# Second layer's recurrence of a hybrid decoder step: key product one slot earlier, output scores in 128-row products, half of the swapping moved to ScalarE

## The reference

```python
def step(s, inp):                      # per token, per head; s is (value, key)
    r_t, lw_t, k_t, v_t, kk_t, a_t = inp
    s_kk = jnp.einsum('bhik,bhk->bhi', s, kk_t)
    s = (s * jnp.exp(lw_t)[:, :, None, :]
         - s_kk[..., :, None] * (kk_t * a_t)[..., None, :]
         + v_t[..., :, None] * k_t[..., None, :])
    return s, jnp.einsum('bhij,bhj->bhi', s, r_t)
```

## Time and profile before

| | |
|---|---|
| median of 3 runs | 1917.25 us (1915.13 to 1920.38) |
| profiled execution | 1919.97 us, span 1918.2 us |
| TensorE busy | 1760.8 us (92%) |
| VectorE busy | 1004.5 us (52%) |
| ScalarE busy | 731.3 us (38%) |
| granted TensorE clock, mean | 0.932 |
| recurrence of layer 2 | about 1089 to 1307 us of the span |

### The profile page before, as it was taken

One profiled execution on the slowest core, in us unless ns is written; L12 is line 12 of the kernel. 1 busy time (PEld: TensorE's weight loads), 2 busy tenths in 40 slices (PEclk: granted clock), 3 DMA queues, 4 the chain that ended last, 5 costly groups with the idle time before them and its releaser, 6 DMA issues.

```text
span 1918.2 us, 42954 instructions
## 1 busy us (share of the span) xinstructions
PE 1760.8 (92%) x18617; PEld 1668.0 (87%) x18617; DVE 1004.5 (52%) x1471; ACT 731.3 (38%) x969; POOL 186.5 (10%) x211
## 2 busy tenths in 40 slices
PE   7999878799999999997999877768899999999997
PEld 6999876799999999996888767765599999999997
DVE  4476774654433444456788556633744442444443
ACT  4353353355522223333466123322445531222343
POOL 1042550000000000110060000012100000000000
PEclk8999988899999999998999867777899999999998
DMA  4322141333332333321222200010143332223321
GB/s 129 89 67 56 47 118 34 88 111 87 92 97 65 87 87 102 103 76 31 69 77 68 67 3 4 4 35 14 28 104 116 87 106 77 70 87 100 87 67 58
DMA packets 234669, 138.95 MB, mean 72 GB/s; under 512 B 4720, under 2 KB 229360, under 8 KB 234528
## 3 DMA queue, kind: packets, MB, share of 16 engines
q1 hardware_dynamic: 226784, 116.73, 21.3%
q0 software_dynamic: 4864, 15.90, 3.3%
q10 hardware_dynamic: 2880, 4.21, 0.6%
HBM read 128.66 MB, written 8.16 MB: 71 GB/s over the span
## 4 chain that ended last, share of the span: by engine, by line
PE 79%; DVE 10%; ACT 5%; issue 3%; POOL 1%; DMA 1%; ACTq 0%; DVEq 0%; SPq 0%; POOLq 0%
PE ps L351 61%; PE ps L2496 2%; PE ps L1881 2%; PE ps L1628 1%; DVE w_rest L320 1%; ACT w_head L315 1%; PE ps L1862 1%; PE ps L1169 1%; POOL mix L984 1%; PE ps L1093 1%; DVE odd_quad L2648 1%; PE ps L2468 1%; PE ps L2775 1%; PE ps L1900 1%; POOL mix L985 0%
## 5 line engine op out<-in xcount | busy, mean ns | idle before, releaser
L351 PE MATMUL ps<-x_split,w_head 128*128 128x272 f32 (+1 forms) x5312 | 897.5, 291 | 25.7 <-DVE x_split L1418 8.5
L351 PEld LDWEIGHTS ps<-x_split,w_head 128*128 128x128 f32 x5312 | 761.4, 191 | 39.8 <-issue 27.4
L351 PE MATMUL ps<-x_split,w_rest 128*128 128x272 f32 (+1 forms) x2656 | 554.3, 290 | 0.0
L315 ACT ACTIVATE w_head<-w_raw 128x1024 fp32r<-128x1024 f32 (+1 forms) x205 | 227.2, 1108 | 582.0 <-PE ps L351 565.4
L351 PEld LDWEIGHTS ps<-x_split,w_rest 128*128 128x128 f32 x2656 | 419.9, 191 | 0.0
L320 DVE TENSOR_TENSOR w_rest<-w_raw,w_head 128x1024 fp32r<-128x1024 f32 (+1 forms) x205 | 268.2, 1308 | 174.3 <-ACT w_head L315 174.2
L351 PE MATMUL ps<-hidden_split,w_head 128*128 128x272 f32 x1408 | 233.1, 287 | 0.0
L351 PEld LDWEIGHTS ps<-hidden_split,w_head 128*128 128x128 f32 x1408 | 198.0, 188 | 0.0
L351 PE MATMUL ps<-hidden_split,w_rest 128*128 128x272 f32 x704 | 145.3, 287 | 0.0
L1459 DVE TENSOR_TENSOR hT<-hT,ps 128x544 f32<-128x544 f32 (+1 forms) x40 | 28.8, 721 | 161.2 <-PE ps L351 161.2
L351 PEld LDWEIGHTS ps<-hidden_split,w_rest 128*128 128x128 f32 x704 | 110.0, 188 | 0.0
(11 more groups left out here) (453 smaller groups left out, 2139.5 us busy)
## 6 DMA issues: line engine op xcount, KB each, us to landing
w_raw<-in_w_ffn_gate SPq DMA_DIRECT2D x44, 512.0 KB, 3.8
w_raw<-in_w_ffn_up SPq DMA_DIRECT2D x44, 512.0 KB, 3.8
w_raw<-in_w_ffn_down SPq DMA_DIRECT2D x32, 704.0 KB, 4.6
w_raw<-in_w_in_even SPq DMA_DIRECT2D x29, 512.0 KB, 3.8
w_raw<-in_w_ple_gate SPq DMA_DIRECT2D x16, 512.0 KB, 4.0
w_raw<-in_w_out_even SPq DMA_DIRECT2D x8, 512.0 KB, 3.9
w_raw<-in_rw_wr SPq DMA_DIRECT2D x8, 512.0 KB, 4.0
w_raw<-in_rw_wk SPq DMA_DIRECT2D x8, 512.0 KB, 3.9
```

Of the source, the lines that this page charges most:

```text
L315: act.activation(wh[:, s, 0:kt * P], raw[:, s, 0:kt * P], ACT.Copy).then_inc(head_ok[s], 1)
L351: mm = pe.matmul(ps[:, 2 * s + h, 0:half.stop - half.start], w[:, s, k * P:(k + 1) * P], x[:, k, half], start=first and k == 0, stop=k == ...
```

## The change

Four things in the recurrence:
- The order of parts is changed. Stream n+2's `aT` is put into slot 1, ahead of U, and its P4 into slot 2. Stream 0 gets one part before the turns of the head begin.
- `O` is 16 products whose stationary tile is 64 rows by 128 columns (both key kinds at once) in place of 32 of 64 by 64.
- The heads' two column halves change places in the inverse tiles (`swap_cols`, `bank(1 - c)`). ScalarE writes the row-swapped half of the inverse beside it (`swapped`), in two copies of 64x128 a level and two of 64x256 at the start. VectorE then transposes `turned_rows`, 128x512, in one instruction a level.
- VectorE's transpose of level x-1 stands in part P of level x, and ScalarE's `first_rows` in part P of level 2.

```diff
+        rows_at = 0, 1792
+        xxs, xTs, aTs = ([quad[:, at + k:at + k + n] for at in rows_at] for k, n in ((0, 512), (768, 512), (1280, 512)))
+        swapped = [quad[:, at + 512:at + 768] for at in rows_at]
+        turned_rows = [quad[:, at + 256:at + 768] for at in rows_at]
...
-            order = ("o", "o", "onoonononon", "no")[slot]
+            order = ("o", "on", "ononononono", "o")[slot]
...
             streams = {m: stream(eng, m) for m in range(SAMPLE + 1)}
+            next(streams[0], None)
...
                 elif kind == "O":
-                    for b in range(2):
-                        for i, p, c in tile_heads:
-                            mm = pe.matmul(bank(c)[half(p ^ b), (2 * i + p) * CP:(2 * i + p + 1) * CP],
-                                           keys_p(2 * i + p, b)[half(c), m, :], qrF[half(c), 2 * i + p, 1, tokens], start=True,
-                                           stop=True)
+                    for i, p, c in tile_heads:
+                        t = 2 * i + p
+                        mm = pe.matmul(bank(c)[:, t * CP:(t + 1) * CP], rows_p[half(c), t, P * m:P * m + P],
+                                       qrF[half(c), t, 1, tokens], start=True, stop=True)
...
-                if kind == "aT":
+                if m < SAMPLE and kind == "P" and x == 2:
                     first_rows(act, m)
...
-            act.activation(xTs[m % 2][:, 0:256], first[:, 0:256], ACT.Copy)
+            act.activation(xTs[m % 2][:, 0:256], first[:, 256:512], ACT.Copy)
             for p in range(2):
-                mm = act.activation(xTs[m % 2][half(p), 256:512], first[half(1 - p), 256:512], ACT.Copy)
+                act.activation(xTs[m % 2][half(p), 256:512], first[half(1 - p), 0:256], ACT.Copy)
+            act.wait_ge(*O2.dve.at(f"t{m}_2"))
+            for p in range(2):
+                mm = act.activation(swapped[m % 2][half(p)], xxs[m % 2][half(1 - p), 0:256], ACT.Copy)
...
+                act.wait_ge(*O2.act.at(f"X{m}_{x}"))
+                for p in range(2):
+                    mm = act.activation(even_columns(swapped[m % 2][half(p)], x),
+                                        even_columns(xxs[m % 2][half(1 - p), 0:256], x), ACT.Copy)
+                mm.then_inc(*O2.act.done(f"x{m}_{x}"))
...
-            dve.wait_ge(*O2.act.at(f"X{m}_{level}"))
-            x, xT = xxs[m % 2], xTs[m % 2]
-            dve.transpose(xT[:, 0:256], x[:, 0:256])
-            for p in range(2):
-                mm = dve.transpose(xT[half(p), 256:512], x[half(1 - p), 256:512])
-            mm.then_inc(*O2.dve.done(f"T{m}_{level}"))
+            dve.wait_ge(*O2.act.at(f"x{m}_{level}"))
+            dve.transpose(xTs[m % 2], turned_rows[m % 2]).then_inc(*O2.dve.done(f"T{m}_{level}"))
...
                 if m < SAMPLE and kind == "P":
+                    if x > 2:
+                        turned_inverse(dve, m, x - 1)
                     level_factor(dve, m, x)
-                elif m < SAMPLE and kind == "X":
-                    if x < LEVELSP:
-                        turned_inverse(dve, m, x)
```

More of the change, by code:

```diff
@@ L2352, in trunk @@
         first = mix[:, 24832:25344]
-        aTs = [quad[:, 2560:3072], quad[:, 0:512]]
-        inverse_at = 512, 1536
-        xxs, xTs = ([quad[:, at + k:at + k + 512] for at in inverse_at] for k in (0, 512))
+        rows_at = 0, 1792
+        xxs, xTs, aTs = ([quad[:, at + k:at + k + n] for at in rows_at] for k, n in ((0, 512), (768, 512), (1280, 512)))
+        swapped = [quad[:, at + 512:at + 768] for at in rows_at]
+        turned_rows = [quad[:, at + 256:at + 768] for at in rows_at]
         aTS, bTS = low2[0][:, 0:P], [low2[0][:, P:2 * P], low2[0][:, 2 * P:3 * P]]
         xTS, xxS, ppS = (low2[1][:, k * P:(k + 1) * P] for k in range(3))
-        sAs = [quad[:, 3328:3840], quad[:, 4864:5376]]
-        sOs = [quad[:, 3840:4864], quad[:, 5376:6400]]
-        vus = [quad[:, at:at + 1024].rearrange("p (i b g v) -> p i b g v", i=4, b=2, g=2) for at in (6400, 7424)]
+        sAs = [quad[:, 3584:4096], quad[:, 5120:5632]]
+        sOs = [quad[:, 4096:5120], quad[:, 5632:6656]]
+        vus = [quad[:, at:at + 1024].rearrange("p (i b g v) -> p i b g v", i=4, b=2, g=2) for at in (6656, 7680)]
         sc_sample = mix[:, 25600:26112].rearrange("p (g n t) -> p g n t", g=2, n=4)
@@ L2371, in head_cols, with swap_cols @@
             return slice(64 * (4 * c + i), 64 * (4 * c + i) + 64)
+        def swap_cols(c, i):
+            return head_cols(1 - c, i)
         def odd_columns(ap, level):
@@ L2446, in pe_stream @@
                     for i, p, c in tile_heads:
-                        mm = pe.matmul(bank(c)[half(1 - p), i * CP:(i + 1) * CP], keys_p(2 * i + p, 1)[half(c), m, :],
+                        mm = pe.matmul(bank(1 - c)[half(1 - p), i * CP:(i + 1) * CP], keys_p(2 * i + p, 1)[half(c), m, :],
                                        qrF[half(c), 2 * i + p, 0, tokens], start=True, stop=True)
@@ L2456, in pe_stream @@
                         r = half(1 - p)
-                        mm = pe.matmul(bank(c)[half(1 - p ^ c), i * CO:(i + 1) * CO], aTs[par][r, head_cols(c, i)],
-                                       even_columns(xxs[par][r, head_cols(c, i)], x), start=True, stop=True)
+                        mm = pe.matmul(bank(1 - c)[half(1 - p ^ c), i * CO:(i + 1) * CO], aTs[par][r, swap_cols(c, i)],
+                                       even_columns(xxs[par][r, swap_cols(c, i)], x), start=True, stop=True)
                 elif kind == "X":
@@ L2493, in pe_inverse @@
                 r = half(1 - p ^ c)
[L2494 to L2497, removed]
+                if x < LEVELSP:
+                    still, moving = xT[r, head_cols(c, i)], even_columns(w[r, swap_cols(c, i)], x)
+                else:
+                    still, moving = w[r, swap_cols(c, i)], odd_columns(xT[r, head_cols(c, i)], x)
+                mm = pe.matmul(bank(1 - c)[half(1 - p), P + i * CO:P + (i + 1) * CO], still, moving, start=True, stop=True)
             return mm
@@ L2596, in act_inverse @@
                     *O2.act.done(f"X{m}_{x}"))
+                act.wait_ge(*O2.act.at(f"X{m}_{x}"))
[3 more added lines that the diff above has]
+                mm.then_inc(*O2.act.done(f"x{m}_{x}"))
                 return
-            made = lambda c: ps[:, bank_of(m, c), P:2 * P].rearrange("p (i s) -> p i s", i=4)
+            made = lambda c: ps[:, bank_of(m, 1 - c), P:2 * P].rearrange("p (i s) -> p i s", i=4)
             act.activation(odd_columns(xTs[m % 2][:, 0:256], x), made(0), ACT.Copy)
```

## The result

The changed kernel takes 1938.02 us, the median of 5 runs (1934.08 to 1939.04); the kernel before takes 1917.25 beside it. The ratio is 1.0105 (95% interval 1.0085 to 1.0125). The forecast was 1914 with a range up to 1925, so the time lies 13 us outside it, on the side of rival 4.

What follows compares the result with a forecast made beforehand. A loop through TensorE, VectorE and ScalarE was taken to set the recurrence's period, no engine being full. Head -1.5, periods -0.6 and chunk 6 -1.2 sum to -3.3: 1919.97 profiled becomes 1916.7, median 1914 us; range 1904 to 1925.

Steps and rivals of the forecast that it cites:

- rival 4: O product: its two row halves don't overlap, +1.8 us in each of 8 chunks, 1928 in all; chance 0.08.
- the O product: In each chunk, 16 products with 64x128 tiles replace 32 of 64x64; put at +0.1 us a period.
- the nearest row: Trace row of the 128*64 form, two tiles at once: 32 records in 1.97 us at low clock, taken for O.
- The walk through the queues: Engine queues of one chunk, timed from its first product `av`: X2' starts at 8.3 us against 8.66, period 20.15.
- The chain of a level: Copies and transpose in one level of the inverse: 1.36 us against 1.42 before, nothing won for one stream.
- Rival 3: ScalarE's string of copies becomes the bound with stalls on top, X2' at 9.4 us, 1923 and more; chance 0.12.
- Head: Before chunk 0, streams 0 and 1 side by side: less VectorE transpose time gives -1.5 us, bounds 0 and -4.1.
- chunk 6: Sample stream's small work runs while X5 is made, shortening the idle before X6: -1.2 us, bounds 0 and -3.4.
- periods: Six stretches from `av` to `av`, chunks 0 to 5: -0.1 us each, -0.6 in all.
- Rival 1: TensorE's clock stays up before X2', so the low phase goes wholly or by half: 1899 or 1906; chance 0.10.

## Why the prediction was wrong

**The step that failed** is the O product: "I take +0.1, by the nearest row". It measured +1.84 a chunk at the low clock, and it carried up to 1.8 more with it, because o and S behind it stayed at half clock. That second cost has no term in the sum: the forecast took the stretch behind O as it was. The nearest row was picked by the wrong likeness. The 128*64 products also have two tiles, but each record loads 64 weight columns; the new O loads 128, and its length does not change when its streamed columns are halved. By weight columns that same row would have given an estimate of 2 x 1.97 = 3.9 us for O, where 3.68 was measured. The kernel before also had a row of the 64*128 form itself, a state transpose of the kind in the earlier trace rows, at a granted clock of 0.50:

```profile
1290.12 1.08 PE L2482 MATMUL ps<-ident,mix 64*128 64x64 f32 x8 [1.79 <-DMA mix<-in_state_rwkv]
```

That is about 110 ns from record to record, near O's 113. These eight are transposes in a single row half, where O's products took 195, so the row warns of the price without explaining it.

Rival 4 (chance 0.08) had the size of O's cost right and its mechanism only in part: its halves were not to overlap at all, and without overlap O is 6.29 us, not 3.7. Its 1928 lacked what the clock added, about 10 us.
The Trainium skill (TensorE: Matmul & The Clock Gate, the section on LDWEIGHTS) says that a weight load's time goes by its columns, at about columns/1.2 ns: for 128 columns an estimate of 107 ns. The alternating order's 113 ns a record at the low clock agrees with it. Other figures here do not: four 64x64 tiles in turn take 28 ns a record, where the rule makes an estimate of 53, and the last O takes 59 ns a record near full clock (0.97), below 107. The measured figures decide, so the rule fits the case of two tiles at the low clock and no more. I had looked only at tile counts.

**The walk through the queues held.** X2' behind `av`: 8.3 foreseen, 8.50 measured, waiting for ScalarE's last swap and not for VectorE. VectorE 2.95 us less busy (2.7), ScalarE 3.09 more (3.2). The chain of a level came out even, as foreseen: 1.40 us from the end of X4's copy (1194.99) to the end of its transpose, where 1.42 was the old chain and 1.36 the foreseen one.

```profile
1195.68 0.71 DVE L2658 STREAM_TRANSPOSE odd_quad<-odd_quad 128x512 f32<-128x512 f32 x1 [1.85 <-ACT odd_quad L2607]
```

With the old O put back, the rest of the change measured 1915.8 against 1916.3 beside it, -0.5, where the sum without O's term was -3.9, just inside the interval (-4.0 to +2.7). Rival 3 (ScalarE's string as the loss, X2' at 9.4) did not happen in the total: X2' came at 8.5.

**Head, chunk 6 and periods**, read in the changed kernel with the old O. Head 31.96 us against 34.96: -3.0, where I took -1.5 with -4.1 as the bound. Chunk 6 22.75 against 24.83: -2.1, where I took -1.2. The six periods 133.5 against 132.5: +1.0, where I took -0.6. In all -4.1 in place of -3.3. That this sum comes out near is partly luck, as the order alone shows. Its head is 33.38, so half of the head's gain came with the order (stream 0's extra part is the likely cause; it was not tested by itself), which had no term, and only 1.4 with VectorE's shorter transposes. Chunk 6 gains as much with the order alone (22.3 to 22.7), as the prediction's reason says. In the periods two errors cancel: the order was worth -7 and the new inverse +8, where each was put near nothing. TensorE's wait before X2' is 2.23 us with the inverse and 1.48 with the order alone, at nearly the same distance from `av` (8.54 and 8.34), since a longer "issue" stall stands ahead of it there (1.41 against 0.68). Why the inverse costs that much in the periods is not shown; the chunks that lengthen most have the lower mean clock (chunks 0 and 1: 0.71 and 0.70 against 0.80 and 0.83).

**The clock** was treated as given by the longest idle time. That was too simple. It fell in every profile, and what differs most between the kernels is when it comes back: o and S run at a granted clock of 0.52 in the changed kernel and of 1.00 with the old O, though the idle time before X2' is 2.23 us in both. Rival 1 (the clock staying up) did not happen, and was not tested on its own.

**What stays open.** Why the exchange of X6 and X2' keeps the clock low for longer in one kernel and not in the other was not settled. I can show that the windows differ by it, but not which of the moved products decides.

## What to carry to other kernels

Halving the number of products by doubling the stationary width can lose time where small tiles already run side by side. Here the weight columns loaded were the same in all and half as many tiles took turns, and 1.99 us became 3.68. Count weight columns and tiles in turn before the number of instructions. In a stage where TensorE swings between its two clock levels, an instruction or a wait inside the half-clock phase can cost its own length and also what it keeps at half clock behind it (1.84 + 1.8 us for O and 1.10 + 1.9 us for the wait, in the chunks shown). And test the parts of a bundled change alone and in pairs: here the order alone gained up to 0.4%, the inverse in the old order lost 0.6% (0.1%, not clear of noise, with the first rows early), and the two together came out even.

## What the runs showed of the hardware

- With stationary tiles of 64 rows by 128 columns in fp32, at half clock, a record takes 113 ns when the row halves alternate, 195 ns in runs of one row half, and 111 ns with 32 in place of 64 streamed columns. Near full clock (0.97) it takes 59 ns, alternating.
- With 64x64 tiles, at half clock, a record takes 28 ns when all four tiles take turns and about 48 ns when only two do, no matter whether they differ in rows or in columns.
- The same 32 records of o take 1.98 us or 1.15 us, by the level of the clock (granted 0.52 or 1.00 over o and S). With 1.84 us less of O ahead of them, or without the wait of 1.10 us, they were at the higher level.
